# Sample stage of a hybrid decoder step: paged and windowed caches taken in steps of three, with two steps loaded ahead

## The reference, cut to what matters

```python
past = kvb_pool[page_table].reshape(B, past_len, 2, H_B, HEAD_DIM)   # 8 sequences x 32 pages of 128 positions
z = jnp.einsum('bqhd,blhd->bhql', q, k) * HEAD_DIM ** -0.5 + sb_bias
log_1m = jnp.where(mask, jax.nn.log_sigmoid(-z), 0.0)
suffix = lax.cumsum(log_1m, axis=3, reverse=True) - log_1m
a = jnp.where(mask, jnp.exp(jax.nn.log_sigmoid(z) + suffix), 0.0)     # stick-breaking weights
o = jnp.einsum('bhql,blhd->bqhd', a, v)
```

## Time and profile before

| | us |
|---|---|
| median of 3 runs | 2216.84 |
| lowest and highest | 2212.31, 2218.42 |
| the profiled execution | 2213.82 |
| its span | 2212.3 |
| PE busy | 1931.0 (87%) |
| DVE busy | 988.3 (45%) |
| ACT busy | 589.7 (27%) |
| POOL busy | 115.0 (5%) |
| mean granted clock of PE | 0.937 |

### The profile page before, as it was taken

How to read it: one execution, slowest core, us unless ns; L and a number is a source line. 1 busy time by engine, 2 the same in 40 slices (tenths; PEclk the granted TensorE clock), 3 DMA queues, 4 the chain that set the end, 5 groups by cost and what they waited for, 6 DMA issues and landing times. The chain is left out here.

```text
span 2212.3 us, 32258 instructions
## 1 busy us (share of the span) xinstructions
PE 1931.0 (87%) x11654; PEld 1630.2 (74%) x11654; DVE 988.3 (45%) x1909; ACT 589.7 (27%) x967; POOL 115.0 (5%) x208
## 2 busy tenths in 40 slices
PE   2699999999677764777786899999999999999995
PEld 2587788999444443554564878999999999999984
DVE  4344111000272873444444736454555455555645
ACT  3100121110473662333222204312211222122212
POOL 0000000000110101333100000000000000000000
PEclk8799999999868876999898999999999999999997
DMA  2844444311551606999672631111111011101102
GB/s 94 320 177 158 159 156 164 154 44 47 165 144 51 213 1 200 340 340 309 264 281 102 230 135 39 49 33 44 57 38 47 28 57 47 39 28 57 38 12 95
DMA packets 134032, 273.98 MB, mean 124 GB/s; under 512 B 23401, under 2 KB 75002, under 8 KB 130042
## 3 DMA queue, kind: packets, MB, share of 16 engines
q1 hardware_dynamic: 112474, 153.93, 20.8%
q0 software_dynamic: 21472, 118.91, 15.2%
HBM read 243.37 MB, written 79.10 MB: 146 GB/s over the span
## 5 line engine op out<-in xcount | busy, mean ns | idle before, releaser
L1913 DVE TENSOR_TENSOR tl_x<-tl_x,tl_ps 128x512 f32<-128x512 f32 (+1 forms) x198 | 135.9, 687 | 207.4 <-PE tl_ps L2070 207.4
L448 PE MATMUL tl_ps<-tl_T_lo,tl_up_hi 128*128 128x364 f32 (+1 forms) x1032 | 227.6, 329 | 0.0
L448 PE MATMUL tl_ps<-tl_T_hi,tl_up_lo 128*128 128x364 f32 (+1 forms) x1032 | 227.6, 329 | 0.0
L448 PE MATMUL tl_ps<-tl_T_hi,tl_up_hi 128*128 128x364 f32 (+1 forms) x1032 | 227.5, 329 | 0.0
L423 PE MATMUL inp_ps<-inp_w_hi,h_hi 128*128 (+1 forms) x432 | 169.5, 392 | 22.8 <-DVE inp_w_lo L382 21.0
L448 PEld LDWEIGHTS tl_ps<-tl_T_hi,tl_up_hi 128*128 128x128 f32 x1032 | 179.1, 188 | 1.4
L448 PEld LDWEIGHTS tl_ps<-tl_T_hi,tl_up_lo 128*128 128x128 f32 x1032 | 178.9, 188 | 0.0
L448 PEld LDWEIGHTS tl_ps<-tl_T_lo,tl_up_hi 128*128 128x128 f32 x1032 | 178.9, 188 | 0.0
L423 PE MATMUL inp_ps<-inp_w_lo,h_hi 128*128 (+1 forms) x432 | 169.1, 391 | 0.0
L423 PE MATMUL inp_ps<-inp_w_hi,h_lo 128*128 (+1 forms) x432 | 168.8, 391 | 0.0
L2070 PE MATMUL tl_ps<-tl_dn_hi,tl_f_hi 128*128 128x512 f32 (+1 forms) x396 | 156.3, 395 | 14.3 <-DVE tl_f_lo L1905 9.4
(11 more groups left out here) (261 smaller groups left out, 3249.3 us busy)
## 6 DMA issues: line engine op xcount, KB each, us to landing
sm_pages<-in_pool POOLq DMA_DIRECT2D x128, 256.0 KB, 4.8
sm_pages<-in_pool SPq DMA_DIRECT2D x128, 256.0 KB, 4.7
out_s<-in_cache POOLq DMA_DIRECT2D x8, 4080.0 KB, 20.8
tl_raw<-in_w_up SPq DMA_DIRECT2D x44, 512.0 KB, 4.6
inp_raw<-in_w_in POOLq DMA_DIRECT2D x10, 2048.0 KB, 9.5
sm_pages<-in_cache SPq DMA_DIRECT2D x16, 1024.0 KB, 9.5
zs<-inp_zt SPq DMA_DIRECT2D x48, 256.0 KB, 4.6
tl_dn_raw<-in_w_down SPq DMA_DIRECT2D x22, 512.0 KB, 3.3
```

What stands on the lines that cost most here:

```text
L448: last = pe.matmul(out[:, n * 512:n * 512 + b - a], lhs, rhs[:, a:b], start=(i == 0), stop=(i == len(pairs) - 1))
L1913: dve.tensor_tensor(x, x, dps[0:n, k * 512:k * 512 + 512], ALU.add).then_inc(added, 1)
```

## The change

- `load_pages` becomes a function of the module, and the page buffers, their semaphores and the page table are split: half of the slots, the table and the semaphores are allocated around both stages. The prompt's stick stage loads the pages of steps 0 and 1: SP after its `rows`, POOL after its wait for them and in front of the copies of the caches.
- In the sample stage SP issues the new rows and the small loads first and then pages from step 2 on; POOL waits for the new rows instead of the table.
- The steps of a sequence stand together: two page steps, then its cache step (`is_stick`). `out` gets three slots.
- On ACT Exp and Ln come ahead of `move(k+1, 0)`, and the Exp of the suffix ahead of `move(k+1, 2)`; in cache steps Exp comes ahead of all moves. On DVE the scan comes ahead of `move(k+1, 1)`, `weights` ahead of `move(k+1, 3)`, `read_out` ahead of `move(k+1, 5)`.
- `turn_out` and `turn_out_shared` of the sequence before run on PE in the first and second page step of a sequence, behind `values(k)`; `place` and `place_shared` run on DVE in the same steps, behind `move_weights(k)`.

```diff
 SQRT = "sqrt_and_others"
+SLOTS = 4
...
             sp.dma_start(bias[:, :], a["sb_bias"].partition_broadcast(P)).then_inc(small_in, 16)
             for t in range(QT):
                 sp.dma_start(rows[:, t, :], zs[t * P:t * P + P, QB:ZC]).then_inc(row_in[t], 16)
+            sp.dma_start(G["table"][:, :], a["page_table"]).then_inc(G["table_in"], 16)
+            sp.wait_ge(row_in[QT - 1], 16)
+            sp.wait_ge(G["table_in"], 16)
+            load_pages(sp, G, a, (0, 1), 0, 2)
             sp.wait_ge(o_done, N)
             sp.dma_start(oTd[:, 2:4, 0:SEQ], oT[:, :, :]).then_inc(o_stored, 16)
             sp.wait_ge(o_stored, 16)
@@ -836,6 +841,8 @@
         def _(pool):
             for t in range(QT):
                 pool.wait_ge(row_in[t], 16)
+            pool.wait_ge(G["table_in"], 16)
+            load_pages(pool, G, a, (2, 3), 0, 2)
             extra_pool(pool)
...
-def sample_stage(nc, K, a, zs, oTd):
+def load_pages(eng, G, a, groups, first, last, consumed=None):
+
+    for k in range(first, last):
+        u, half = k % SLOTS, k % 2 * (PAGES // 2)
+        pages = G["pages"][u // 2]
+        if k >= SLOTS:
+            eng.wait_ge(consumed, k - SLOTS + 1)
+        for g in groups:
+            if k % 3 < 2:
+                at = k // 3 * PAGES + PAGES // 2 * (1 - k % 3) + 4 * g
+                with eng.Fori(0, 4) as j:
+                    page = eng.value_load(G["table"][0:1, ds(j + at, 1)], min_val=0, max_val=NPOOL - 1)
+                    eng.dma_start(pages[:, ds(j + (half + 4 * g), 1), :],
+                                  a["pool"][ds(page, 1), :, :].rearrange("a p c -> p a c")).then_inc(G["page_in"][u][g], 16)
+            else:
+                b = k // 3
+                src = (a["cache2"][b].rearrange("(k r) c -> k r c", r=4),
+                       a["cache3"][b].rearrange("(k r) c -> k r c", r=16)[:, 0:4, :],
+                       a["cache3"][b].rearrange("(k r) c -> k r c", r=16)[:, 4:8, :],
+                       a["cache1"][b].unsqueeze(1))[g]
+                eng.dma_start(pages[:, half + 4 * g:half + 4 * g + (4 if g < 3 else 1), :], src).then_inc(G["page_in"][u][g], 16)
+
...
         STEPS = STICK + NB
-        ROUNDS = STEPS // SLOTS
-        pages = s.sb("pages", [P, SLOTS * HALF, 512])
-        table = s.sb("table", [1, NB * PAGES], I32)
+        G["pages"].append(s.sb("pages", [P, 2 * HALF, 512]))
         bias, bias_z, fold = s.sb("bias", [P, 1]), s.sb("bias_z", [P, 1]), s.sb("fold", [P, C])
         after, same = s.sb("after", [P, P]), s.sb("same", [P, P])
...
         vnew = s.sb("vnew", [P, NB, 256])
         tbank, zbank, obank = s.psum("tbank", 1024), s.psum("zbank", 1024), s.psum("obank", 512)
         abank, xbank, ybank = s.psum("abank", 512), s.psum("xbank", 512), s.psum("ybank", 512)
-        page_in = [[s.sem(f"page_in{u}{g}") for g in range(4)] for u in range(SLOTS)]
-        rows_in, table_in, small_in, own_in, vnew_in = (s.sem(n) for n in ("rows_in", "table_in", "small_in", "own_in", "vnew_in"))
...
-            sp.wait_ge(table_in, 16)
-            load_pages(sp, (0, 1))
+            load_pages(sp, G, a, (0, 1), 2, STEPS, v_done)
             sp.wait_ge(x_done, 4 * 2 * NB)
...
         @block.gpsimd
         def _(pool):
-            pool.wait_ge(table_in, 16)
-            load_pages(pool, (2, 3))
+            pool.wait_ge(rows_in, 16)
+            load_pages(pool, G, a, (2, 3), 2, STEPS, v_done)
...
             for k in range(STEPS):
                 u, more = k % 2, k + 1 < STEPS
-                if k < STICK:
+                if is_stick(k):
+                    m = stick(k)
+                    v = m % 2
+                    act.wait_ge(z_done, k + 1)
+                    act.activation(odds[:, u, :], odds[:, u, :], ACT.Exp, scale=SCALE).then_inc(odds_done, 1)
+                    act.wait_ge(odds_done, m + 1)
+                    if m >= 2:
+                        act.wait_ge(scanned, m - 1)
+                    act.activation(soft[:, v, :], odds[:, u, :], ACT.Ln, bias=1.0).then_inc(soft_done, 1)
                     if more:
                         move(act, k + 1, 0)
-                    act.wait_ge(z_done, k + 1)
-                    act.activation(odds[:, u, :], odds[:, u, :], ACT.Exp, scale=SCALE).then_inc(odds_done, 1)
-                    act.wait_ge(odds_done, k + 1)
-                    if k >= 2:
-                        act.wait_ge(scanned, k - 1)
-                    act.activation(soft[:, u, :], odds[:, u, :], ACT.Ln, bias=1.0).then_inc(soft_done, 1)
-                    if more:
-                        move(act, k + 1, 2)
-                    act.wait_ge(scanned, k + 1)
-                    if k >= 2:
-                        act.wait_ge(a_done, k - 1)
-                    act.activation(left[:, u, :], suffix[:, u, :], ACT.Exp, scale=-1.0).then_inc(left_done, 1)
-                    if more:
-                        move(act, k + 1, 4)
-                        move(act, k + 1, 6)
-                    act.wait_ge(nbias_done, k + 1)
-                    act.wait_ge(o_done, max(0, k - 1))
-                    act.activation(factor[:, u:u + 1], nbias[:, u:u + 1], ACT.Exp).then_inc(factor_done, 1)
-                else:
-                    if more:
-                        move(act, k + 1, 0)
-                    act.wait_ge(nm_done, k - STICK + 1)
-                    if k >= STICK + 2:
-                        act.wait_ge(share_done, k - STICK - 1)
-                    act.activation(odds[:, u, :], odds[:, u, :], ACT.Exp, bias=nm[:, u:u + 1], scale=SCALE,
-                                   accum_out=den[:, u:u + 1]).then_inc(a_done, 1)
+                    act.wait_ge(scanned, m + 1)
+                    if m >= 2:
+                        act.wait_ge(a_done, k - 2)
+                    act.activation(left[:, v, :], suffix[:, v, :], ACT.Exp, scale=-1.0).then_inc(left_done, 1)
                     if more:
                         move(act, k + 1, 2)
                         move(act, k + 1, 4)
                         move(act, k + 1, 6)
-                    act.wait_ge(peak_done, k - STICK + 1)
+                    act.wait_ge(nbias_done, m + 1)
+                    if k >= 2:
+                        act.wait_ge(o_done, k - 1)
+                    act.activation(factor[:, u:u + 1], nbias[:, v:v + 1], ACT.Exp).then_inc(factor_done, 1)
+                else:
+                    b = k // 3
+                    w = b % 2
+                    act.wait_ge(nm_done, b + 1)
+                    if b >= 2:
+                        act.wait_ge(share_done, b - 1)
+                    act.activation(odds[:, u, :], odds[:, u, :], ACT.Exp, bias=nm[:, w:w + 1], scale=SCALE,
+                                   accum_out=den[:, w:w + 1]).then_inc(a_done, 1)
+                    if more:
+                        for e in range(0, 8, 2):
+                            move(act, k + 1, e)
+                    act.wait_ge(peak_done, b + 1)
                     act.wait_ge(o_done, k - 1)
-                    act.activation(factor[:, u:u + 1], peak[:, u:u + 1], ACT.Exp).then_inc(factor_done, 1)
+                    act.activation(factor[:, u:u + 1], peak[:, w:w + 1], ACT.Exp).then_inc(factor_done, 1)
...
 
             for k in range(STEPS):
                 more = k + 1 < STEPS
-                if k < STICK:
+                if is_stick(k):
                     exponents(k)
+                    suffix_sums(k)
                     if more:
                         move(dve, k + 1, 1)
-                    suffix_sums(k)
+                    weights(k)
                     if more:
                         move(dve, k + 1, 3)
-                    weights(k)
+                    if k:
+                        read_out(k - 1)
                     if more:
                         move(dve, k + 1, 5)
                         move(dve, k + 1, 7)
-                    if k:
-                        read_out(k - 1)
                     carried(k)
-                    if k % 2 == 1 and k >= 3:
-                        place(k // 2 - 1)
                     move_weights(k)
+                    if k >= 3:
+                        (place if k % 3 == 0 else place_shared)(k // 3 - 1)
                 else:
                     maxima(k)
                     if more:
@@ -1337,13 +1356,9 @@
                     read_out(k - 1)
                     tops(k)
                     move_weights(k)
-                    if k == STICK:
-                        place(NB - 1)
-                    if k >= STICK + 2:
-                        place_shared(k - STICK - 2)
                     peaks(k)
+            place(NB - 1)
             read_out(STEPS - 1)
-            place_shared(NB - 2)
             place_shared(NB - 1)
...
             new_rows()
@@ -1504,24 +1520,20 @@
             for k in range(STEPS):
                 if k + 1 < STEPS:
                     turn(k + 1)
-                if k < STICK:
+                if is_stick(k):
                     carry(k)
                 else:
```

(56 more changed lines are left out.)

142 lines of the change are left out of this document (72 added, 70 removed).

## The result

The changed kernel takes 2226.3 us (median of 5 runs, 2223.1 to 2227.6), the kernel before, run beside it, 2215.5 (2212.3 to 2218.4). The ratio is 1.0043, 95% interval 1.0029 to 1.0057. The forecast was 2226, slower by 0.4%. The profiled execution took 2224.1 us, span 2222.5; that of before 2213.8.

The account below looks back on a forecast made before the run. It took the sample stage's chain of scores, exponents, functions and copies as the bound, not loads. Steps -4, start -2 and low clock +15 gave +9 us: 2213.8 to 2223 profiled, 2226 as median; range 2196 to 2262.

Parts of the forecast that it names:

- The bound: Sample stage: the chain of scores, exponents, functions and copies sets its time; PE's page waits are only 6.0 us.
- The rival at 2170: Sample stage: the loads were the bound after all, so it falls by some 45 us, to 2170; chance 0.08.
- The hold: DVE's `place` and `place_shared` wait for PE's turns: exponents 6.4 us, maxima 6.15 us after the scores; fourteen holds.
- The page step in the new order: Stick step, exponents to scores: 8.4 us, 8.8 behind a cache step; first three steps, without holds, 30.7 us.
- The group: Two page steps and their cache step: 15.2, 14.15 and 9.9 us, together 39.2 us before the clock's cost.
- The clock term: PE idles 2.6 us in each of fourteen holds, then runs at low clock: 1.1 us each, +15 us.
- the first rival: The low clock stays through the cache step behind each group's second hold: +43 us, 2269 us; chance 0.2.
- The sign of being wrong: Three steps under 37 us, no holds in the chain, a clock low over 10 us in each group, or page waits.
- Loads ahead: Pages of steps 0 and 1 load in the prompt stage at no cost there; PE waits for no page.
- The start: Start of the sample stage, where PE waits 12.0 us for its rows: 2 us saved, at most about 6.
- The tail: After the last step, to the last store: 12 us, about 10.4 in the kernel before.
- The rival "copies don't wait for the scan": Stick steps: copies start earlier, sixteen steps save 1.2 us each, -25 us in all, 2192 us; chance 0.15.

Follow-up runs that it names:

- e1: The changed kernel with `place` and `place_shared` one step later on DVE, behind the next step's read-out; 2178.0 us, ratio 0.9828.
- e12: The changed kernel with PE running `turn_out` and `turn_out_shared` in front of the next scores instead of behind the values; 2170.1 us, ratio 0.9789.
- e9: The changed kernel with only `place` moved behind the next step's read-out, `place_shared` left in front of the maxima; 2203.7 us, ratio 0.9940.
- e3: The changed kernel with 16 added PE transposes of constants ahead of the third group in held steps and in cache steps; 2226.2 us, ratio 1.0032.
- e4: The changed kernel with the pages of steps 0 and 1 loaded in the sample stage, not ahead; 2227.9 us, ratio 1.0064.
- e10: The kernel of e1 with the pages of steps 0 and 1 loaded in the sample stage, not ahead; 2180.0 us, ratio 0.9843.
- e8: The changed kernel with the pool queue's wait for the new rows taken out; 2236.8 us in one run.
- e11: The kernel of e1 with the last stick sequence's `turn_out` in front of the last step's value products; 2177.7 us, ratio 0.9821.
- e2: The changed kernel with the old order of copies and functions in page steps; 2221.1 us, ratio 1.0030.
- e7: The changed kernel with the edits of e1 and e2 together: late placing and the old order of copies; 2201.4 us, ratio 0.9916.
- e5: The kernel before with `turn_out` behind `values` in even steps, `place` behind `weights`, `place_shared` one step later; 2198.1 us, ratio 0.9912.
- e6: The kernel of e1 with page loads for the first eight steps only, later steps using what stands in the slots; 2178.15 us in one run.

## Why the prediction was right, and which terms were off

- **The bound** (the chain, not the loads): right, and shown from both sides. With one hold of two out, about half of the gain comes (groups 37.2 between 41.15 and 34.1); with the loads gone from e1, nothing moves. The rival at 2170 named a time that e12 reaches, for another reason.
- **The hold**: forecast 6.4 and 6.15 us from scores to exponents and maxima, measured 6.26 and 6.03. (The terms given for the first, 1.7, 1.9, 1.8 and 0.8, add up to 6.2.) Both waits are where they were put, fourteen in all. That they cause the time is shown by e1, e9 and e12, each of which takes the wait away from another side.
- **The page step in the new order**: 8.8 forecast behind a cache step, 8.7 measured; the first three steps 30.7, measured 30.9.
- **The group**: 39.2 and 2.2 for the clock, 41.4; measured 41.15. The clock term was right as a mean and wrong in shape: four groups lie 0.7 to 1.4 us above 39.2 (0.3 of it is a cache step that takes 10.2 at full clock, not 9.9), two 3.7, where the clock is at 0.70 as far as the next group's exponents. That is the first rival at half its price, in two groups of six. The sign of being wrong, a low clock for over 10 us, is met by these two (an estimated 17 us each, from granted clocks of 0.69 and 0.70); by the same estimate two others come to about 10 and the last two to 7. The price can be read off the two pairs of stretches above: 16.6 less 14.9 us for a granted clock of 0.69 in place of 0.89. e3 was to show it by experiment and didn't, so the clock's share rests on those rows.
- **Loads ahead**: forecast nothing in the prompt stage and no page waits; measured, the prompt's stick stage is no longer than before (140.5 and 141.7 us), the pages are issued from 726 to 749 us, and PE waits for none. Right; e4 and e10 put the worth at 2 us.
- **The start**: mis-sized. Forecast -2 us; from the `bias` issue to the first exponents it is 33.5 after and 33.6 before, and PE's wait for the rows is 11.6 after 12.0. I read the wait for rows as a contest with the pool's pages. It is not: behind the rows stands a chain of small steps, and the guard only keeps it as it was (e8).
- **The tail**: mis-sized. Forecast 12 us from the last maxima to the store, measured 16.0. The rows above have part of the reason: clock 0.56 there. At half clock the 32 last value products took 3.79 us, and in e1, with a mean clock of 0.89, the same tail but for one shared turn took 13.7. So some 2.3 of the 4 us are clock, which I had charged to the holds alone; the other 1.7 lies in what stands in series behind the values. For a turn and a place I had added 1.6 us to the tail of before (12 less 10.4), and moving the turn alone gives 2.3 back (e11). Start and tail are 1.2 and 4 us too short in the sum, the groups 3.5 too long (six at 0.25, and the last, whose 29.6 us up to the maxima I had with the clock at 31.5). So the profiled execution came out at 2224.1 where the sum said 2223: the closeness is in part two errors that cancel.
- **The rival "copies don't wait for the scan"**: its effect exists but in the other place: the new order costs 1.2 us in the first step (10.4 us, 9.2 in e2), as forecast, and 0.75 us a group more than the old one where the holds stand (41.15 and 40.4).

The rows of before would have allowed more than the forecast of a loss: the two rows that carried the hold name the edit that takes it out. The Trainium skill says as much (Perfetto Trace Analysis, Optimization Strategy): find the gaps of the engine and make what ends them start sooner. The trace agrees in e12, 2170 us by moving one PE step. The same section's other advice, that mixing regimes may help, is not borne out here: e7 and e5, mixed and not, with the same order of copies in the page steps, have the ratios 0.9916 and 0.9912, and the loads bound neither kernel.

## What to carry to other kernels

When a change puts a step that waits for another engine in front of the operation the next step starts with, price the wait from the order of that other engine; it can swallow everything the change was good for. Judge a reordering with the waits around it gone: the same order of copies was worth -3 and +20 us here. And try the parts of a change one by one, since here only one of them gave anything. A small write-out belongs behind the next step's urgent work, or its producer in front of it: either end of the wait can be moved, and the producer's end gave more. A transfer share of 0.96 is no proof of a bound; leave the loads out once and look.

## What was not expected of the hardware

Transfers at 351 GB/s into the buffers that PE reads beside them cost the engines nothing that the trace can show: in e1 and e6 PE was busy 59.31 and 59.30 us, DVE 38.77 and 38.77, with and without them.

The stage in front of this one has two lengths in the same code. From its own `bias` issue to that of the sample stage the changed kernel took 140.5 us (712.45 to 852.90), e1, equal up to there, 146.7 (710.55 to 857.28), e11 148.3. It isn't the loads ahead: the kernel before took 141.7, and e5, which is the same there, 146.6, in these two stretches, e5 first:

```profile
712.00:850.00 138.00, 98.00 (x616) 64.06 (x616) 93.32 (x128) 82.22 (x144) 7.71 (x16) 0.75 0.29 97
```

```profile
712.00:850.00 138.00, 91.99 (x624) 61.16 (x624) 93.25 (x129) 83.16 (x145) 7.72 (x16) 0.79 0.30 102
```

The longer one has PE at a lower granted clock, 0.75 for 0.79, and busy 6 us longer. What decides between them stays open. It is why stages are compared here rather than spans, and 5 us is what it adds to or takes from a profiled execution.

Transposes alone kept the full clock: in e12 PE ran 5.3 us of little else, between value products and scores, and was granted 1.00.

```profile
1045.40:1050.70 5.30, 4.38 (x37) 3.44 (x34) 2.07 (x3) 2.27 (x6) 2.67 (x5) 1.00 0.98 342
```

The Trainium skill's TensorE: Matmul & The Clock Gate (Part 4) says that full clock doesn't engage for transposes, which don't count as busy in the same way. In these stretches the trace disagrees: besides the row above, in the changed kernel the granted clock was 0.50 from 1073.5 to 1076.2 and rose to 1.00 while PE ran nothing but 20 transposes (1072.66 to 1076.90).

Left open: e12 with `place` late as well, or with the earlier last turn, was not run, and neither was the kernel before with nothing but the new order of copies and its holds out.
